# The first block's attention scores as three float32r products of split queries and keys

## The reference

```python
def attend(qblk):
    logits = jnp.einsum('bqhd,bkhd->bhqk', qblk, k).astype(jnp.float32) * SM_SCALE
    p = jax.nn.softmax(logits, axis=-1).astype(v.dtype)
    return jnp.einsum('bhqk,bkhd->bqhd', p, v)
```

## Time and profile before

| | |
|---|---|
| median of 3 runs | 3762.04 us (3758.5 to 3762.19) |
| the profiled execution | 3755.82 us, of it 3754.5 us span |
| mean granted TensorE clock | 0.981 |
| PE busy | 3559.0 us, 95% |
| DVE busy | 2185.6 us, 58% |
| ACT busy | 1531.7 us, 41% |
| attention of layer 0, first scores to last sums | 196.74 to 411.61 us |
| attention of layer 1, first scores to last sums | 1196.38 to 1366.03 us |

### The profile page before, as it was taken

The page is one execution under the profiler, slowest core; times in us unless marked ns, Lnnn a source line. Parts: engine busy times, 40 slices in busy tenths (PEclk is TensorE's granted clock), DMA queues, the critical chain, the costliest instruction groups (busy, mean ns, idle before and its releaser), DMA issues.

```text
span 3754.5 us, 49718 instructions
## 1 busy us (share of the span) xinstructions
PE 3559.0 (95%) x20631; PEld 3007.7 (80%) x20631; DVE 2185.6 (58%) x3641; ACT 1531.7 (41%) x2278; POOL 482.4 (13%) x421
## 2 busy tenths in 40 slices
PE   7998999999989988999889999999999998999999
PEld 5755778888876557887678788799999998988899
DVE  3275463333374746445655434478999885666666
ACT  3245532221234464222454533333567674333332
POOL 0000000000000000000000011002332344343340
PEclk9999999999999999999999999999999999999999
DMA  6400112333302002222221153247787899988884
GB/s 251 163 2 1 57 57 102 123 113 113 113 35 82 1 34 79 98 94 96 107 78 40 57 162 109 87 150 261 266 281 247 286 329 351 333 321 313 325 324 160
DMA packets 123570, 581.56 MB, mean 155 GB/s; under 512 B 13984, under 2 KB 31504, under 8 KB 82384
## 3 DMA queue, kind: packets, MB, share of 16 engines
q1 hardware_dynamic: 67744, 365.46, 27.1%
q0 software_dynamic: 55600, 212.91, 16.0%
HBM read 516.97 MB, written 61.34 MB: 154 GB/s over the span
## 4 chain that ended last, share of the span: by engine, by line
PE 74%; DVE 13%; ACT 7%; DMA 3%; issue 3%; POOL 0%; SPq 0%; DVEq 0%; ACTq 0%; POOLq 0%
PE ps L667 20%; PE ps L668 19%; PE ps L669 19%; DVE WL L538 2%; PE ps L3217 2%; PE ps L1420 2%; DVE ACC L1621 2%; PE ps L570 1%; DVE MX L1594 1%; DVE OH L2956 1%; DVE UB L3052 1%; ACT WH L528 1%; PE ps L2350 1%; PE ps L1499 1%; DMA gdram<-GST 1%
## 5 line engine op out<-in xcount | busy, mean ns | idle before, releaser
L538 DVE TENSOR_TENSOR WL<-stage,WH 128x2048 fp32r<-128x2048 f32 x239 | 546.0, 2285 | 336.5 <-ACT WH L528 328.9
L667 PE MATMUL ps<-HH,WH 128*128 128x512 f32 (+1 forms) x1672 | 619.8, 371 | 24.0 <-DVE HL L993 16.2
L528 ACT ACTIVATE WH<-stage 128x2048 fp32r<-128x2048 f32 x239 | 455.2, 1905 | 392.0 <-PE ps L669 358.0
L668 PE MATMUL ps<-HL,WH 128*128 128x512 f32 (+1 forms) x1672 | 611.3, 366 | 0.0
L669 PE MATMUL ps<-HH,WL 128*128 128x512 f32 (+1 forms) x1672 | 608.4, 364 | 0.0
L667 PE MATMUL ps<-HP,WH 128*128 128x384 f32 (+1 forms) x1088 | 381.6, 351 | 9.8 <-DVE WL L538 8.5
L667 PEld LDWEIGHTS ps<-HH,WH 128*128 128x128 f32 x1672 | 317.3, 190 | 89.1 <-issue 28.3
L668 PE MATMUL ps<-LP,WH 128*128 128x384 f32 (+1 forms) x1088 | 375.1, 345 | 0.0
L669 PE MATMUL ps<-HP,WL 128*128 128x384 f32 (+1 forms) x1088 | 374.8, 344 | 0.0
L669 PEld LDWEIGHTS ps<-HH,WL 128*128 128x128 f32 x1672 | 316.4, 189 | 53.9
L668 PEld LDWEIGHTS ps<-HL,WH 128*128 128x128 f32 x1672 | 317.3, 190 | 50.6 <-issue 1.2
(11 more groups left out here) (475 smaller groups left out, 5851.1 us busy)
## 6 DMA issues: line engine op xcount, KB each, us to landing
stage<-in_w SPq DMA_DIRECT2D x64, 1024.0 KB
stage<-in_u SPq DMA_DIRECT2D x64, 1024.0 KB
stage<-in_v SPq DMA_DIRECT2D x64, 1024.0 KB
stage<-in_w_mod SPq DMA_DIRECT2D x40, 1024.0 KB
adram<-GA SPq DMA_DIRECT2D x128, 192.0 KB
gdram<-GST SPq DMA_DIRECT2D x24, 1024.0 KB, 9.2
GR<-gdram POOLq DMA_DIRECT2D x32, 768.0 KB
AR<-adram POOLq DMA_DIRECT2D x32, 768.0 KB
```

The source lines that it names most:

```text
L528: act.e.activation(k.WH[o % 2][:, 0:w], k.stage[n % 2][:, 0:w], ACT.Copy).then_inc(*act.done("slab_hi", n))
L538: dve.e.tensor_tensor(k.WL[o % 2][:, 0:w], k.stage[n % 2][:, 0:w], k.WH[o % 2][:, 0:w].bitcast(F32), ALU.subtract).then_inc(*dve.done("sla ...
L667: pe.e.matmul(o, wh[:, kk, cs], L.view(L.hh, kk, z), start=first, stop=False)
L668: pe.e.matmul(o, wh[:, kk, cs], L.view(L.hl, kk, z), start=False, stop=False)
```

## The change

The scores of the first block are made of rounded halves. Four new steps prepare them, and one list of steps orders them:

- DVE copies the 32 rotary rows of the keys, rounded to float32r, into the high halves of both key buffers (`kr_high`) and writes the rests into the low halves (`kr_copy`). Before it made two plain copies.
- ACT's copy of the 64 projected rows of a head's keys (`k_head`) now rounds them into `KH`. In a new step "low" DVE subtracts them from PSUM into `KL` (`k_low`, 64x768). The step stands at the end of the unit with part 0, ahead of that unit's last "behind" steps. The PSUM tile of the keys is now freed by `k_low`.
- A new part 3 of "head", in the unit after part 2 (the last unit of a head): after the rotary sum ACT rounds the queries into `QH` (`q_high`, 96x768 in layer 0, 96x512 in layer 1), and DVE subtracts (`q_low`), writing the rest over the query itself (`QL` has the address of `QR`).
- PE's scores wait for `k_low` and `q_low` and are three float32r matmuls for each float32 one, for 512 and for 256 keys.

`KH` and `QH` lie in `WH` and `WL` of the pair of split buffers that is free in that layer (pair 0 in layer 0, pair 1 in layer 1), for two heads. No memory is added. Before the loop, "low" of head 0 stands behind the first "v" and part 3 of head 0 behind part 2.

```diff
...
@@ -258,12 +258,19 @@
     k.HL = h.tensor("HL", [128, 8, 768], FR)
     homes = [at + 8192, at + 24576] + [y_at + 8192 * i for i in range(3)] + [r.at + 8192 * i for i in range(3)]
     k.first = [nc.alloc_sbuf_tensor_at(f"first{n}", [128, SLAB], F32, offset=o) for n, o in enumerate(homes)]
-    new = Room(nc, z.at).tensor
+    room = Room(nc, z.at)
+    new = room.tensor
     k.WQ = new("WQ", [128, 2, 768])
     k.tda = [new(f"TDa{i}", [96, 512]) for i in range(2)]
     k.V = new("V", [128, 6, 512])
+    low_at, high_at = room.at, [at, at + 8192]
+    k.ql = [nc.alloc_sbuf_tensor_at(f"QL{i}", [96, 768], FR, offset=low_at + 3072 * i) for i in range(2)]
     k.qr = [new(f"QR{i}", [96, 768]) for i in range(2)]
-    k.kr = [new(f"KRr{i}", [96, 768]) for i in range(2)]
+    k.kl = [new(f"KL{i}", [96, 768], FR) for i in range(2)]
+    k.kh = [[nc.alloc_sbuf_tensor_at(f"KH{l}{i}", [96, 768], FR, offset=high_at[l] + 3072 * i) for l in range(2)]
+            for i in range(2)]
+    k.qh = [[nc.alloc_sbuf_tensor_at(f"QH{l}{i}", [96, 768], FR, offset=high_at[l] + 16384 + 3072 * i) for l in range(2)]
+            for i in range(2)]
     k.pb = [new("Pb", [128, 768])] + k.g2
     k.ptb = [new(f"PTb{i}", [128, 768]) for i in range(2)]
     k.ot = [new(f"OT{i}", [128, 768]) for i in range(2)]
@@ -1336,12 +1343,15 @@
     per = len(units) // 8
     scored, turned, outs, pairs, head, done = [], [], [], [], [], 0
     yield "head", (0, 0)
-    for tt in range(4):
+    yield "v", 0
+    yield "low", 0
+    for tt in range(1, 4):
         yield "v", tt
     yield "head", (0, 1)
     yield "v", 4
     yield "v", 5
     yield "head", (0, 2)
+    yield "head", (0, 3)
     for n, u in enumerate(units + [None, None, None]):
         ended = pairs.pop(0) if pairs else None
         if outs:
@@ -1353,9 +1363,10 @@
             yield "scores", u
             scored.append(u)
             if n % per == per - 4 and u[0] + 1 < 8:
-                head = [(u[0] + 1, part) for part in range(3)]
-        if head:
-            yield "head", head.pop(0)
+                head = [(u[0] + 1, part) for part in range(4)]
+        now = head.pop(0) if head else None
+        if now:
+            yield "head", now
         if behind:
             yield "behind", behind.pop(0)
         if ended is not None:
@@ -1368,6 +1379,8 @@
             yield "values", v
             if v[1] == units[-1][1]:
                 outs.append(v[0])
+        if now and now[1] == 0:
+            yield "low", now[0]
         if ended is not None:
             yield "scaled", ended
         for _ in range(1 if l == 0 else 2):
@@ -1412,12 +1425,15 @@
         elif kind == "scores":
             h, q0, k0, kn = u
             p = k.psum.take(pe, ("s", l, u), ("p_exp", (l, u)))
-            qb, kb = k.QR.of((l, h)), k.KRr.of((l, h))
-            pe.wait_ge("k_head", (l, h))
+            (_, qh, ql), (kl, kh), qs = k.QR.of((l, h)), k.KRr.of((l, h)), slice(q0, q0 + 128)
+            pe.wait_ge("k_low", (l, h))
             pe.wait_ge("kr_copy", l)
-            pe.wait_ge("roped", (l, h))
+            pe.wait_ge("q_low", (l, h))
             for (s0, sn) in ([LAT, CTX] if kn == 768 else [(0, 256)]):
-                mm = pe.e.matmul(p[:, s0:s0 + sn], qb[:, q0:q0 + 128], kb[:, k0 + s0:k0 + s0 + sn], start=True, stop=True)
+                o, ks = p[:, s0:s0 + sn], slice(k0 + s0, k0 + s0 + sn)
+                pe.e.matmul(o, qh[l][:, qs], kh[l][:, ks], start=True, stop=False)
+                pe.e.matmul(o, ql[:, qs], kh[l][:, ks], start=False, stop=False)
+                mm = pe.e.matmul(o, qh[l][:, qs], kl[:, ks], start=False, stop=True)
             mm.then_inc(*pe.done("scores", (l, u)))
         elif kind == "turn":
             p, pb = k.psum.take(pe, ("t", l, u), ("p_turned", (l, u))), k.Pb.of((l, u))
@@ -1484,7 +1500,7 @@
 def tensor_head(k, pe, l, h, part):
     segs = both(l)
     if part == 0:
-        p = k.psum.take(pe, ("kh", l, h), ("k_head", (l, h)))
+        p = k.psum.take(pe, ("kh", l, h), ("k_low", (l, h)))
         pe.wait_ge("kv_normed", l)
         pe.wait_ge(f"wkv{l}", 0)
         for (s0, sn) in (LAT, CTX):
@@ -1499,10 +1515,10 @@
                 mm = pe.e.matmul(p[0:96, s0:s0 + sn], k.WQ[:, kk, 96 * h:96 * h + 96], k.ZQ[:, kk, s0:s0 + sn],
                                  start=(kk == 0), stop=(kk == 1))
         mm.then_inc(*pe.done("q_mm", (l, h)))
-    else:
+    elif part == 2:
         p = k.psum.take(pe, ("rot", l, h), ("rope_s", (l, h)))
         pe.wait_ge("q_head", (l, h))
-        pe.e.matmul(p[0:96, 0:512], k.rotM[:, :], k.QR.of((l, h))[:, 0:512], start=True,
+        pe.e.matmul(p[0:96, 0:512], k.rotM[:, :], k.QR.of((l, h))[0][:, 0:512], start=True,
                     stop=True).then_inc(*pe.done("rot", (l, h)))
 
 
@@ -1518,16 +1534,19 @@
             h, part = u
             end = ("scores", (l, (h, att_last(l)) + ((512, 256) if l == 0 else (0, 768))))
             if part == 0:
-                kb = k.KRr.take(act, (l, h), end)
-                act.wait_ge("kr_copy", l)
+                kh = k.KRr.take(act, (l, h), end)[1][l]
                 act.wait_ge("k_mm", (l, h))
-                act.e.activation(kb[0:64, :], k.psum.of(("kh", l, h))[0:64, 0:768],
+                act.e.activation(kh[0:64, :], k.psum.of(("kh", l, h))[0:64, 0:768],
                                  ACT.Copy).then_inc(*act.done("k_head", (l, h)))
             elif part == 1:
-                qb = k.QR.take(act, (l, h), end)
+                qb = k.QR.take(act, (l, h), end)[0]
                 act.wait_ge("q_mm", (l, h))
                 act.e.activation(qb[:, a:b], k.psum.of(("qh", l, h))[0:96, a:b], ACT.Copy,
                                  scale=SM).then_inc(*act.done("q_head", (l, h)))
+            elif part == 3:
+                q, qh, _ = k.QR.of((l, h))
+                act.wait_ge("roped", (l, h))
+                act.e.activation(qh[l][:, a:b], q[:, a:b], ACT.Copy).then_inc(*act.done("q_high", (l, h)))
         elif kind == "scores":
             n = att_count(l) * u[0] + u[1] // 128
             pb = k.Pb.take(act, (l, u), ("turned", (l, u)))
@@ -1582,12 +1601,26 @@
     if l == 0:
         vector_mod_close(k, dve, 0, 21)
     dve.wait_ge("roped", (l, "k"))
-    for buf in k.kr:
-        i = dve.e.tensor_copy(buf[64:96, :], k.KR[64:96, :])
+    for kh in k.kh:
+        i = dve.e.tensor_copy(kh[l][64:96, :], k.KR[64:96, :])
+    i.then_inc(*dve.done("kr_high", l))
+    dve.wait_ge("kr_high", l)
+    for kl, kh in zip(k.kl, k.kh):
+        i = dve.e.tensor_tensor(kl[64:96, :], k.KR[64:96, :], kh[l][64:96, :].bitcast(F32), ALU.subtract)
     i.then_inc(*dve.done("kr_copy", l))
     for kind, u in att_order(l):
-        if kind == "head" and u[1] == 2:
-            vector_rope(k, dve, k.QR.of((l, u[0])), ("rot", l, u[0]), (l, u[0]))
+        if kind == "low":
+            kl, kh = k.KRr.of((l, u))
+            dve.wait_ge("k_head", (l, u))
+            dve.e.tensor_tensor(kl[0:64, :], k.psum.of(("kh", l, u))[0:64, 0:768], kh[l][0:64, :].bitcast(F32),
+                                ALU.subtract).then_inc(*dve.done("k_low", (l, u)))
+        elif kind == "head" and u[1] == 2:
+            vector_rope(k, dve, k.QR.of((l, u[0]))[0], ("rot", l, u[0]), (l, u[0]))
+        elif kind == "head" and u[1] == 3:
+            q, qh, ql = k.QR.of((l, u[0]))
+            dve.wait_ge("q_high", (l, u[0]))
+            dve.e.tensor_tensor(ql[:, a:b], q[:, a:b], qh[l][:, a:b].bitcast(F32),
+                                ALU.subtract).then_inc(*dve.done("q_low", (l, u[0])))
         elif kind == "scores":
             m = att_count(l) * u[0] + u[1] // 128
             dve.wait_ge("scores", (l, u))
...
-    k.G2, k.KRr, k.QR = ring(k.g2), ring(k.kr), ring(k.qr)
+    k.G2, k.KRr, k.QR = ring(k.g2), ring(list(zip(k.kl, k.kh))), ring(list(zip(k.qr, k.qh, k.ql)))
```

More of the change, by code:

```diff
@@ L50 @@
     "sums": ("moments", "rows_mm"),
-    "att_evicted": ("k_head", "q_head", "v", "p_exp", "p_turned", "o_out", "sum_rows", "silu"),
+    "att_evicted": ("k_head", "q_head", "q_high", "v", "p_exp", "p_turned", "o_out", "sum_rows", "silu"),
     "heads_evicted": ("kvc", "rope_raw", "rope_sq", "rope_ln", "rope_rstd", "vsw", "gate_rows", "gate", "dv", "hid_rows", "hid", "kz", "vcm"),
@@ L63 @@
     "convolved": ("tap", "conv", "centered", "conf_normed"),
-    "att_rows": ("row_max", "recip", "o_scaled", "rope_s", "rope_c", "roped", "kr_copy"),
+    "att_rows": ("row_max", "recip", "o_scaled", "rope_s", "rope_c", "roped", "kr_high", "kr_copy", "k_low", "q_low"),
     "mix_rows": ("z_dve", "m_lo", "relu_sq", "act_lo", "down"),
```

## The result

| | before | after |
|---|---|---|
| median | 3762.11 us (4 runs, 3758.5 to 3763.72) | 3803.43 us (4 runs, 3794.61 to 3807.53) |
| profiled execution | 3755.82 us, span 3754.5 us | 3794.61 us, span 3793.3 us |
| mean granted clock | 0.981 | 0.975 |

What follows compares the result with a forecast made beforehand. PE and DVE were both near full in attention, the lead changing within a head. Losses of 12.3 + 11.5 + 4 + 3.1 + 5 = 35.9 us on 3755.8 gave 3791.7, plus 6.2 for the median: 3798 us, range 3772 to 3822.

Steps and rivals of the forecast that it cites:

- the clock: Half clock behind the added PE gaps in attention: 5 us taken, bounds 0 and 27 us, mostly hidden by DVE's lead.
- the untapped preparations: Two head preparations without convolution taps in each layer: 1 us lost each, 4 us in all, nearer to nothing.
- Query split: Head's last unit: maximum, exponential, q_high, q_low in a row; next maximum 2.35 us later in layer 0, 2.3 in layer 1.
- Key split: Keys' subtraction mostly fits DVE's idle time: 0.3 us a head in layer 0, nothing in layer 1.
- Starts: Before each layer's first scores q_high and q_low stand uncovered: 1.8 us in layer 0, 1.3 in layer 1, 3.1 in all.
- rival 3: Half clock paid in full at fourteen gaps and more: 24 us in place of 5, 3817 us; chance 20%.
- The savings: Cheaper score products on PE: 0.23 us per 768-key unit, at most 16.1 us in all, real only where PE leads.
- (1): PE leads throughout and the split steps find cover: 16.1 us saved less 3.1, some 3749 us; chance 5%.
- (2): DVE's waits are taken back in its idle time later in the head: 3762 to 3769 us; chance 8%.
- (4): Float32r scores of 96 rows no faster than float32, or buffer notes don't hold: about 5 us above forecast; chance 2%.

Runs made afterwards that it cites:

- experiment 3: Changed kernel plus up to three overwritten dummy float32 products before a head's first scores, so PE does not stand idle; 3790.43 us.
- Experiment 2: Changed kernel without the keys' low half and its subtraction; the third product takes the high half again; 3799.94 us.
- experiment 1: Changed kernel without the queries' low half and rounding copy; the high half is used twice, so PE keeps three products; 3761.22 us.
- experiment 9: Changed kernel with neither query nor key split; all three float32r products take the high halves; 3760.15 us.
- experiment 4: Changed kernel with all splitting and waits kept, but scores made as one plain float32 product of the high halves; 3811.07 us.
- experiment 11: Kernel before the change with only the convolution taps dealt differently over the units of a head; 3753.42 us.
- experiment 5: Changed kernel with q_high and q_low moved one unit earlier, to the end of the unit with the rotary sum; 3779.24 us.
- experiment 6: Changed kernel with only q_low moved, behind the first tap of its unit; 3802.67 us.
- experiment 7: Changed kernel with both query steps one unit earlier and the query subtraction on GpSimd for all heads but the first; 3784.65 us.
- experiment 10: Changed kernel with both query steps one unit earlier, taps dealt differently over a head's units, and the keys' subtraction behind its unit's last taps; 3783.54 us.

## Why the prediction was right, and where it was wrong

The forecast was 36 us above the median before, and it came out 41 above. The mechanism of the larger part is the one forecast: a chain from maximum to `q_low` in a stretch that DVE leads. The sum came near partly by luck, since errors offset each other: the clock came out 7 to 8 us dearer than its term, the untapped preparations 3.5 us cheaper. The stated range also reaches lower than its parts: 3798 - 4 - 5 - 12 is 3777 us, not 3772. For the terms I compare with the kernel of experiment 3, which has the clock of before: its span is 26.9 us above before, where my terms without the clock made 30.9.

- **Query split, tapped preparations.** Right in place, order and price. DVE idle before `q_low`: forecast 1.4 us, measured 1.36. PE idle before the first scores: "over 3 us", 3.36. Maximum to maximum 2.35 us later forecast, 2.66 measured, of which 0.25 is DVE's new wait for scores at half clock. Heads of 23.9 and 18.9 us forecast, 24.30 and 19.94 measured, 23.88 and 18.88 without the half clock. Attention of about 232 and 185 us forecast, 230.67 and 190.65 measured.
- **Key split.** Forecast 0.3 us a head in layer 0 and none in layer 1. Experiment 2 took 3.5 us off the median, too little to tell from nothing with these intervals. The wait behind ACT's copy was forecast at 0.8 us in layer 0; over seven heads it is 6.6 us, 0.94 each. In layer 1 it was about a microsecond, and is 9.6 us, 1.4 each. There the forecast was nothing ("it fits"), and experiments 1 and 9 show 3.0 us. In experiment 3 a query product (at 255.01) waits 0.36 us for `k_low`, as forecast.
- **Starts.** 1.8 us forecast for layer 0, and PE's wait before the first scores grew from 2.26 to 4.03 us. 1.3 us forecast for layer 1, and it grew from 2.26 to 3.55 us.
- **Layer by layer, clock aside.** From the first query product to that of the seventh head (the start and five tapped preparations) before takes 134.1 us in layer 0 and 98.3 in layer 1, experiment 3 takes 146.7 and 113.3. That is 12.6 us more for my 14.1, and 15.0 for my 12.8. In layer 1 the first of the five costs more than the others. From a head's first maximum to the next head's it is 18.64 us against 15.12 before, 3.5 us more, where a plain head has 2.3 us more. The extra 1.2 us lie in the unit of the keys' subtraction, 1217.54 - 1212.52 = 5.02 us from maximum to maximum against 1202.21 - 1198.39 = 3.82. Before had 0.84 us of DVE's idle time there, and the wait and the subtraction need 2.24:

```profile
1215.22 0.95 DVE L1620 TENSOR_TENSOR KL<-ps,KH 64x768 fp32r<-64x768 f32 x1 [1.29 <-ACT KH L1544]
```

- **Untapped preparations.** Forecast 4 us. From the seventh query product to the end of attention experiment 3 takes 88.6 and 78.4 us, before 88.4 and 78.2: 0.5 us for all four (before rounding), about my lower bound of nothing. In the changed kernel these stretches take 90.8 and 81.5 us, 5.7 us more than before, and 5.2 of them go with the clock.
- **The clock: the step that failed.** "I take 5 us, near nothing because DVE leads right behind these gaps." It is 12 to 13 us. Of 15 gaps of over 1.4 us that PE spends waiting for a low half, 12 have a stretch at half clock at their end or within 2 us behind it, so about 1 us for each. The loss of speed itself was sized well: 1.7 us a place, and about 23 us in all. What was mis-sized is how much of it DVE's lead hides. It is half and not most. In the layer 0 head 0.4 us is paid of 24.30 x (1 - 0.93) = 1.7, in the layer 1 head 1.1 us of 19.94 x (1 - 0.91) = 1.8, and in the untapped stretches 5.2 us is paid. The Trainium skill, "TensorE: Matmul & The Clock Gate", section "HAM oscillation", has each burst behind a long idle stretch start slow. The trace agrees for the longer gaps: all ten of over 3 us are followed by a stretch at half clock (0.52 in the window shown), and two of the five shorter ones. (The forecast's "every added gap pays" left out that the section speaks of long ones.) But with all of it paid the time would have been rival 3's 3817 us. The rule told where it happens, not what of it is paid.
- **The savings.** 0.24 us a unit measured, 0.23 forecast. That they buy nothing where DVE leads was right for most of them (experiment 9: 4.8 us of 16.1 in the windows). In the changed kernel they come out at 7.6 to 11.5 us (experiment 4). That the half clock makes them worth more there is likely, but not shown.
- **Rivals.** (1) PE leads: false; even with neither split the time is that of before. (2) Waits taken back: false, PE's idle time grew by 38.1 of the 38.8 us. (3) Of the 19 us that it put on top of my clock term, 7 to 8 came true. (4) float32r no faster with 96 rows: false, 1.15 us against 1.39 us a unit.

Could any order save the change? In its layer 0 head DVE works 20.12 us and in its layer 1 head 16.07 us. The heads of experiment 11 are 20.22 and 15.78 us long in all. So even with DVE never idle the split kernel would only be level with that one; experiments 5, 6, 7 and 10 tried four placements, and the best stood 16.5 us above before. That bound holds for heads with twelve taps each. Taps dealt over all eight heads would lower DVE's load in the first five, and this was not tried: over the whole of layer 0's attention DVE is busy 143.89 of 230.67 us.

## What to carry to other kernels

When two engines are each near full in a stage, find out which leads at each point of a period, not on average: work taken off the one that is ahead buys nothing, and work or waits put on the other cost in full. A rounding split in a chain that ends in the first use costs the chain, not the operation: here 0.95 us of subtraction became 2.66 us. A gap also costs what the clock loses behind it, here about 1 us for each gap. If both engines are close, deal the movable work so that each unit's load fits the leader first; here that alone gave 8 us with no new operation.

## What was not expected of the hardware

A subtraction on GpSimd with both inputs in SBUF stops DVE's taps nearly for its length: 1.80 us of POOL, 3.67 us for two taps that otherwise take 2.09. Over the 60 taps of layer 0 the mean went from 1028 ns (experiment 5) to 1147 ns (experiment 7):

```profile
L1656 DVE SCALAR_TENSOR_TENSOR ACC<-U,cols,ACC 128x784 f32<-128x784 f32 x60 | 61.7, 1028 | 0.8
```

```profile
L1658 DVE SCALAR_TENSOR_TENSOR ACC<-U,cols,ACC 128x784 f32<-128x784 f32 x60 | 68.8, 1147 | 0.8
```

Of seven subtractions five lie beside these taps. Three of them stretch a pair of taps as shown above, and two stretch a pair like this one:

```profile
267.10 3.32 DVE L1658 SCALAR_TENSOR_TENSOR ACC<-U,cols,ACC 128x784 f32<-128x784 f32 x2
```

Together they cost DVE 68.8 - 61.7 = 7.1 us, 1.4 us each, more than a subtraction on DVE itself (0.95 us). The Trainium skill, "SBUF — State Buffer", section "Who interferes with whom", says that a VectorE instruction with two inputs in SBUF contends with a GpSimd instruction that reads SBUF. A tap has two such inputs, and the trace agrees.

The other surprise is that a half-clock stretch can follow a short gap. In layer 0's two heads with pair work PE stood idle 1.51 us. Behind the one that ended at 271.6 us the clock fell, behind the one that ended at 321.6 us it did not:

```profile
271.60:276.00 4.40, 4.39 (x24) 3.47 (x25) 4.33 (x5) 1.27 (x3) 0.00 (x0) 0.69 0.00 0
321.60:326.00 4.40, 4.08 (x30) 3.10 (x32) 4.33 (x5) 1.27 (x3) 0.00 (x0) 1.00 0.00 0
```
